# First transfers issued before the branch, rotary tables copied within SBUF, own blocks loaded after the weights, query products ordered by piece of tokens

## The reference

```python
u = rmsnorm(h, ln1_g)
z = u @ w_in                    # zb|zc|zv (3 x 1024), q_lat 768, kv_lat 512, k_rope 64, gates 2 x 2048
y_conv = (zb * causal_dwconv3(zc * zv, conv_w)) @ w_conv_out
q = (rmsnorm(q_lat, q_a_g) @ w_q_b)       # 16 heads of 128 + 64
k, v = (rmsnorm(kv_lat, kv_a_g) @ w_kv_b) # 16 heads of 128 and 128, k_rope shared by the heads
q, k = rope(rmsnorm(q)), rope(rmsnorm(k)) # cos and sin of position * inverse frequency
h = h + (sigmoid(ga) * y_conv + sigmoid(gb) * causal_attention(q, k, v) @ w_mla_out) @ w_o
h = h + (silu(a_g) * a_u) @ w_down,  a = causal_dwconv3(rmsnorm(h) @ w_up) + b
```

## Time and profile before

| | us |
|---|---|
| median of 3 runs | 2425.15 |
| the profiled execution | 2420.54 |
| its span on the slowest core, 6 | 2418.9 |
| TensorE busy in it | 2350.9 (97%) |
| VectorE, ScalarE busy | 1342.5 (56%), 1094.9 (45%) |
| granted clock of TensorE, mean over core 6's span | 0.996 |

### The profile page before, as it was taken

The page is one execution under the profiler, slowest core; times in us unless marked ns, Lnnn a source line. Parts: engine busy times, 40 slices in busy tenths (PEclk is TensorE's granted clock), DMA queues, the critical chain, the costliest instruction groups (busy, mean ns, idle before and its releaser), DMA issues.

```text
span 2418.9 us, 41748 instructions; the slowest of 8 cores (2401.0 to 2418.9 us)
## 1 busy us (share of the span) xinstructions
PE 2350.9 (97%) x13850; PEld 1245.6 (51%) x13900; DVE 1342.5 (56%) x2585; ACT 1094.9 (45%) x1876; POOL 172.8 (7%) x330
## 2 busy tenths in 40 slices
PE   4989999999999999999999999999999999999999
PEld 2875555555555555544444444444444444444444
DVE  3772777777777777761111111277467457547742
ACT  4863788888788888861111113433023113213310
POOL 1000000000000000000000000000100100110011
PEclk9999999999999999999999999999999999999999
DMA  8654121212020202144554466454454455455457
GB/s 210 177 96 79 20 40 24 40 19 50 14 50 14 50 10 50 51 98 90 83 82 80 83 136 160 70 88 78 75 92 81 74 91 88 68 90 88 79 107 155
DMA packets 66053, 189.10 MB, mean 78 GB/s; under 512 B 7520, under 2 KB 23136, under 8 KB 64672
## 3 DMA queue, kind: packets, MB, share of 16 engines
q0 software_dynamic: 46944, 140.56, 35.5%
q1 hardware_dynamic: 18880, 45.67, 5.5%
HBM read 311.80 MB, written 14.51 MB: 135 GB/s over the span
## 4 chain that ended last, share of the span: by engine, by line
PE 94%; DMA 2%; DVE 1%; issue 1%; ACT 1%; SPq 0%; DVEq 0%; ACTq 0%; POOLq 0%
PE ps L612 94%; ACT arena L619 1%; DMA arena<-wkvin 1%; DMA arena<-wall 1%; DVE arena L630 1%; DVE arena L626 1%; SPq L646 0%; SPq L205 0%; ACT L619 0%; DVEq L183 0%; ACTq L183 0%; DVE arena L643 0%; SPq L210 0%; POOLq L183 0%; SPq L212 0%
## 5 line engine op out<-in xcount | busy, mean ns | idle before, releaser
L612 PE MATMUL ps<-arena 128*128 128x476 bf16 (+5 forms) x13850 | 2350.9, 331 | 63.7 <-DMA arena<-xg 18.9
L612 PEld LDWEIGHTS ps<-arena 128*128 128x128 bf16 x13900 | 1245.6, 98 | 1168.8 <-issue 79.6
L630 DVE TENSOR_TENSOR arena<-arena 128x478 f32<-128x478 f32 (+19 forms) x1292 | 640.8, 537 | 224.5 <-ACT arena L619 202.0
L630 DVE TENSOR_TENSOR arena<-ps,arena 128x476 f32<-128x476 f32 (+6 forms) x558 | 330.0, 591 | 770.2 <-PE ps L612 745.2
L619 ACT ACTIVATE arena<-arena 128x476 f32<-128x476 f32 (+9 forms) x543 | 378.1, 712 | 682.0 <-DVE arena L630 603.7
L619 ACT ACTIVATE arena<-ps,arena 128x476 bf16<-128x476 f32 (+6 forms) x832 | 491.2, 632 | 406.8 <-PE ps L612 373.6
L626 DVE SCALAR_TENSOR_TENSOR arena<-arena 128x476 f32<-128x476 f32 (+8 forms) x603 | 358.0, 609 | 47.0 <-ACT arena L619 25.4
L619 ACT ACTIVATE arena<-ps 128x512 bf16<-128x512 f32 (+7 forms) x496 | 268.3, 561 | 119.8 <-PE ps L612 116.1
L646 POOL DMA_DIRECT2D arena<-wall x302 | 159.4, 528 | 2112.0 <-PE ps L612 2048.0
L626 DVE SCALAR_TENSOR_TENSOR arena<-ps,arena 128x256 bf16<-128x256 f32 (+1 forms) x65 | 26.9, 464 | 5.2 <-ACT arena L619 4.1
L646 POOL DMA_DIRECT2D arena<-xg x23 | 12.7, 563 | 119.1 <-PE ps L612 53.5
(11 more groups left out here) (3 smaller groups left out, 0.3 us busy)
## 6 DMA issues: line engine op xcount, KB each, us to landing
arena<-wall POOLq DMA_DIRECT2D x182, 512.0 KB, 5.4
arena<-wall POOLq DMA_DIRECT2D x48, 320.0 KB, 4.2
arena<-xg SPq DMA_DIRECT2D x9, 1024.0 KB, 9.1
arena<-wall POOLq DMA_DIRECT2D x32, 256.0 KB, 3.9
arena<-xg POOLq DMA_DIRECT2D x15, 512.0 KB, 9.2
arena<-xo SPq DMA_DIRECT2D x16, 477.0 KB, 13.9
outT<-arena SPq DMA_DIRECT2D x31, 238.0 KB, 5.2
arena<-wall POOLq DMA_DIRECT2D x32, 224.0 KB, 5.6
```

Source lines behind the costliest of these rows:

```text
L612: S.add(PE, lambda e: e.matmul(out, lhsT=lhsT, rhs=rhs, start=start, stop=stop), reads, writes, cost=max(width(rhs) / 2400.0, 0.055) + 0.003)
L630: S.add(DVE, lambda e: e.tensor_tensor(out=out, in0=in0, in1=in1, op=op), reads, writes, cost=dcost(out, in0, in1) + held)
```

## The change

Five things change.

1. `cst`, the first seven chunks of `wkvin` (SyncE) and the eight pieces of pair 0 (GpSimd) are marked `pre` and issued ahead of the read of `which`. They must be the same in all shares, so the tile of pair 0 now lies at the start of the region and the staging tiles behind it. `posg`, which differs by share, follows after the branch, with chunk 7.
2. The tables are copied from `tS` and `tC` straight into `CS`, 16 transfers of 32 partitions each (4 quarters x 4 groups of rows). `cs_d` is gone. `rope(g)` waits only for the quarters it reads.
3. `oload(0)` and all later own blocks are asked for once chunk 15 of `wkvin` has been. The first two weights of ring `A` are asked for by `prefetch`, when the first `NST` own blocks have been asked for, and their transfers wait until the last of those has landed.
4. Query products go by pieces: blocks 0 to 3 of piece 0, of piece 1 and so on, then blocks 4 and 5; each reads only the columns of `u_own` of its piece (`Tup`). `krstat` of the last pair, and `kvstat` when the number of pairs is odd, move in among them, and the convolution begins when all query products are done. Small tiles are placed ahead of the later x tiles.
5. `NXB` (tiles for pairs) becomes 2 where a share has late own blocks (share 0), and the cap on `NST` rises from 6 to 7. By the sizes, share 0 goes from 4 and 5 tiles to 2 and 7; share 1 keeps 4 and 5, share 2 keeps 4 and 4, share 3 keeps 3 and 4.

```diff
@@ Sched.replay
-    def replay(self, e, eng, eng_sem, chan_sem, final_waits):
+    def replay(self, e, eng, eng_sem, chan_sem, final_waits, pre=False):
         for o in self.ops[e]:
+            if o.pre != pre:
+                continue
@@ emit
     def body(e, eng):
+        progs[0][0].replay(e, eng, eng_sem, chan_sem, (), pre=True)
         v = eng.value_load(which[0:1, 0:1])
@@ the first transfers
-    dma(SP, posi, posg[:, 0:QW], "pos", writes=[Tposi])
     dma(SP, cst, cstd[:, 0:NC_CONST - 128], "cst", writes=[Tcst])
...
-    for k in range(8):
-        if k < NWS:
-            wload(k)
-        if k % 2:
-            for h in range(2):
-                xpiece(0, h, 4 * (k // 2), 4)
+    for k in range(7):
+        wload(k)
+    for k in range(4):
+        for h in range(2):
+            xpiece(0, h, 4 * k, 4)
+    for e in (SP, POOL):
+        for o in S.ops[e]:
+            o.pre = True
+    dma(SP, posi, posg[:, 0:QW], "pos", writes=[Tposi])
+    if NWS > 7:
+        wload(7)
@@ sine, csload
         act(dst, q, AF.Sin, [Tq], [Tdst])
-        x = 1 - which
-        dma(SP, cs_d[128 * x:128 * x + 128, 0:QW], dst, "csw%d" % x, reads=[Tdst], writes=[Tcsd[x]])
-        if which == 0:
-            return
-        csload(0, 1)
-        oload(0)
-
-    def csload(q0, q1):
+        F1.mark("sin", which)
+
+    def csload(q):
 
         for r in (2, 3, 0, 1):
-            x = 0 if r < 2 else 1
-            dma(SP, CS[32 * r:32 * r + 32, QW * q0:QW * q1].rearrange("p (q n) -> p q n", n=QW),
-                cs_d[128 * x + 32 * q0:128 * x + 32 * q1, 0:QW].rearrange("(q p) n -> p q n", p=32), "cs%d%d" % (q0, r),
-                reads=[Tcsd[x]], writes=[TCSall[4 * (q0 > 0) + r]])
-        F1.mark("tab", q0)
+            v, Tv = (tC, TtC) if r < 2 else (tS, TtS)
+            dma(SP, CS[32 * r:32 * r + 32, QW * q:QW * q + QW], v[32 * q:32 * q + 32, :], "cs%d%d" % (q, r),
+                reads=[Tv], writes=[TCSall[4 * q + r]])
+        F1.mark("tab", q)
@@ units of the first stage
-        if i > 0:
+        if 0 < i < 5:
+            for q in [i - 1] if sh.first else range(4) if i == 1 else ():
+                f_d.units.append(Unit(lambda q=q: csload(q), 0.0, pos=-9.0, ok=lambda q=q: at("sin") >= 1 and (q == 0 or at("old") >= 0)))
+        if True:
             f_d.units.append(Unit(lambda i=i: oload(i), 0.0, pos=-9.0,
-                                  ok=lambda i=i, g=g, c=c: (not c or at("ld%d" % (g - 1)) > 0) and at("old") >= i - 1 and at("own") >= i - NST
+                                  ok=lambda i=i, g=g, c=c: at("w") >= 15 - NWS and (not c or at("ld%d" % (g - 1)) > 0) and at("old") >= i - 1 and at("own") >= i - NST
                                   and at("cast") >= sh.ncast[max(i - NST + 1, 0)] - 1))
-        if i == 1:
-            f_d.units.append(Unit(lambda: csload(1, 4), 0.0, pos=-9.0, ok=lambda: at("ld%d" % min(3, NG - 1)) > 0 and at("tab") >= 0))
@@ buffers, prefetch
-    NXB = 4 if spare > 7 else 3
-    NST = min(spare - NXB, 6)
+    NXB = 2 if sh.late else 4 if spare > 7 else 3
+    NST = min(spare - NXB, 7)
...
+    def prefetch():
+
+        wlimit["A"] = 2
+        wbehind.extend(t for t in Txo[min(NST, len(sh.own)) - 1:] if not t.dead)
+        wpump()
+        wbehind.clear()
@@ query products
-    def ql(i, t):
+    qseq = [(i, t) for b in (range(4), range(4, 6)) for t in range(NT) for i in b]
+
+    def ql(m):
+        i, t = qseq[m]
...
-            mm(PS[p][:, 0:n], wv[:, k, :], u_own[:, k, 2 + off:2 + off + n], k == 0, k == 15, [Tw, Tu[k]], [TP[p]])
+            mm(PS[p][:, 0:n], wv[:, k, :], u_own[:, k, 2 + off:2 + off + n], k == 0, k == 15, [Tw, Tup[k][t]], [TP[p]])
...
     NQ = 6 * NT
     for n in range(NQ):
-        if n == 4:
+        if n == 2 and NG % 2:
+            st_l.units.append(Unit(lambda: kvstat(NG - 1), 0.45, need=[Tsqkv[2 * ((NG - 1) % 2) + 1]], pos=-9.0))
+        if n == 5:
+            st_l.units.append(Unit(last_krstat, 0.12, need=[Tsqkr[(NG - 1) % 2]], pos=-9.0))
             st_l.units.append(Unit(krot, 0.0, pos=-9.0))
```

More of the change, by code:

```diff
@@ L645, in dma @@
     def dma(eng, out, in_, chan, reads=(), writes=()):
[L646 to L647 removed]
+        o = S.add(eng, lambda e: e.dma_start(out=out, in_=in_), reads=reads, writes=writes, chan=chan,
+                  cost=in_.shape[0] * width(in_) * esz(in_.dtype) / 2.7e5)
+        if o:
+            o.where = repr((out, in_))
     def rsq(out, ssq, n, reads, writes):
```

113 lines of the change are left out of this document (68 added, 45 removed).

## The result

The changed kernel is slower, not faster. Its time is that of the kernel before times 1.0028, with a 95% interval of 1.0016 to 1.0039, so about 7 us lost where I forecast 4 gained. The other five lie between 2427.4 and 2431.6, with a median of 2430.8.

The account below looks back on a forecast made before the run. TensorE's products were taken as the work, with only idle time to save, mainly in the front that ScalarE's chunk scaling ends. Front 2.6 plus query products 1.2 made 3.8 us off 2425.15: 2421 us, range 2412 to 2429.

Parts of the forecast that it names:

- Of 7.9 us of lead 2.6 are left: Front, core 6: transfers start 7.9 us sooner, but sines waiting for `posg` leave a gain of 2.6 us.
- 1.2 us gained: Query products, core 6: placed between the last pair's two statistics, they remove TensorE's 1.16 us wait; 1.2 us gained.
- `posg` begun at 9.7, landed at 22: Front, SyncE's queue: `posg` begun at 9.7 us, asked for at 12.3, landed behind seven chunks at 22.
- rival 3: Branch: the far share's code is fetched through full queues, `posg` lands at 29.9, 4.1 us slower, 2429; chance 0.15.
- under the wait: Front: squares of pair 0, its mean square and a 1.28 us table change hidden while ScalarE waits for the sines.
- The last chunk at 42.5: Front, ScalarE: sines at 30.4 and 36.4 us, last `wkvin` chunk scaled at 42.5 instead of 45.1.
- It follows at a fixed distance: End of front: with the last chunks scaled, TensorE has all operands of its first pair and follows at a fixed distance.
- nothing loses: Own blocks behind the weights: `oload(0)` some 9 us sooner, pair loads move no more than the last chunk; 0 us.
- Tables without DRAM: 0, own blocks: nothing: Front: 832 KB less traffic against six more issues, 2.5 us of SyncE's time; both costed at nothing, as were own blocks.
- The hole at 134 us: 0: TensorE's idle stretch from VectorE's queue of own blocks: left unchanged, 0, with 8.1 us the most it could give.
- Rival 4: Hole at 134 us: the front's 2.6 us are waited away there and only 1.2 stay, 2424; chance 0.15.
- Rival 2: Front: `posg` overtakes the chunks or lands near 15 us, the full 7.9 us arrive, 2416 or 2414; chance 0.25.

Follow-up runs that it names:

- experiment 9: Changed kernel with the squares of the query products put in the buffers in turn, not in their piece's buffer: ratio 1.0008 [0.9998, 1.0018], 2424.4 us.
- nine other kernels with the same beginning: Nine follow-up kernels that begin like the changed kernel, first transfers ahead of the read of `which`; `posg` asked for at 16.6 to 20.9 us on core 6.
- experiment 3: Kernel before with only the first transfers moved ahead of the read of `which`, `posg` after the branch: ratio 1.0014 [1.0003, 1.0025], 2427.1 us.
- experiment 1: Changed kernel with `which` read first, then the shared first transfers, still ahead of the branch: ratio 1.0040 [1.0025, 1.0054], 2432.5 us.
- experiment 5: Changed kernel with both sines on ScalarE behind the last of the sixteen scaled chunks: ratio 0.9978 [0.9967, 0.9989], 2417.7 us.
- the four kernels of the second table: Changed kernel; kernel before with early transfers alone; changed kernel with old query order; changed kernel with squares in turn: 100th weight load 10.9 to 11.4 us after last chunk.
- experiment 4: Changed kernel with the old order of query products, their banks, and the last pair's statistics back in the first stage: ratio 1.0003 [0.9992, 1.0014], 2424.8 us.
- experiment 2: Changed kernel without its first part: transfers back behind the branch, `posg` first, the rest kept: a single time, 2425.3 us, no interval.
- experiment 12: Kernel before with both sines behind the sixteen chunks: ratio 1.0027 [1.0015, 1.0039], 2430.1 us.
- experiment 13: Kernel before with the first transfers ahead of the branch and both sines behind the chunks: two times, 2421.3 and 2422.5 us, no interval.
- experiment 14: Changed kernel with first transfers back behind the branch, sines behind the chunks, squares in turn: ratio 0.9980 [0.9969, 0.9991], 2416.7 us.
- the first four rows of the table: Changed kernel as is, with squares in turn, with sines last, and with both: +7.5, +3.6, -7.1, -6.4 us against the kernel before at weight load 100.
- experiment 8: Changed kernel with `which` first, old query order, pair 1 asked for sooner, and whole `posg` among the first transfers: ratio 0.9968 [0.9954, 0.9981], 2414.4 us.
- experiment 10: Changed kernel with both sines behind the chunks and the squares of the query products in turn: ratio 0.9952 [0.9938, 0.9967], 2410.4 us.

## Why the prediction was wrong, point by point

Two steps of the sum failed. "Of 7.9 us of lead 2.6 are left" was about -1.9 us (experiment 9, ratio 1.0008, with an interval that reaches to none), and "1.2 us gained" by the query products was -5. The time lies nearly 2 us above my range.

**The lead itself.** Right: the first chunk was asked for at 1.52 us (forecast 1.6), `xg` at 1.56. SyncE was through with its chunks at 7.8, not 4.5: issues of 0.42 us grew to 1.63 as the queue filled. That is 3.3 us of the loss of `posg`.

**`posg` begun at 9.7, landed at 22.** From the load of `which` to the first issue in the branch I took the 5.2 us of empty queues; it was 22.43 - 7.82 = 14.6, and the landing was at 26.7. In this execution 8.1 of the 9.4 us that were added are in the read of `which` (9.38 - 1.33) and 1.4 in the jump (4.71 - 3.34). With the 3.3 us above, less the 2.58 us stall of the first issue that didn't come (0.33 now), that makes the 10.1 us between 12.3 and 22.43. In the nine other kernels with the same beginning it is the other way round: in eight of them the read grew by 0.6 to 2.2 us, and the stretch from its end to `posg` more, from 3.8 to between 6.3 and 8.0. So rival 3, the far branch through full queues, had a real mechanism, and I gave it 0.15. What it added to the read of `which` it didn't name. Its threshold, a landing at 25.8, was not what decides: experiment 3 loses 3 us with a cast at 24.9.

By the rule weighed there (the Trainium skill, "Advanced Engine Details and Errata", Control Flow Timing, about 108 ns for a compare-and-branch) the jump would be next to nothing; the trace disagrees again, with 4.71 us.

**The cast follows the landing.** I had VectorE start when `posg` is there. But the sum of pair 0's squares now stands ahead of the cast in its order, and waits for pair 0's last pieces. In experiment 1, and in six of the nine kernels above, the cast waits for that sum and not for `posg`. I had said that squares, mean square and table change lie "under the wait". Only the mean square does: the squares hold the cast, sums of squares put between make the 8.4 us to the angle 9.3 (26.82 to 36.16), and the table change of 1.28 us comes when the angle is there and adds to the chain. So the first sine ran at 37.46 in the profiled execution and at 34.43 in experiment 9, not at 30.4.

**The last chunk at 42.5.** It was 48.8 in the profiled execution and 44.6 in experiment 9. The chain was the right one, ScalarE's fixed order, as experiment 5 shows; its inputs were off.

**"It follows at a fixed distance", and "nothing loses".** This is the step that failed in kind. I took the last chunk as the end of the front, had TensorE follow it at the old distance, and let the pair loads move "by no more than the last chunk does". The distance grew from 7.1 us to about 11 in the four kernels of the second table with the lead and the sines between the chunks, also where the last chunk came sooner than before: in experiment 4 it is done 1.5 us sooner, and the 100th weight load 2.8 us later. While the sines hold the chunks, no chunk is reloaded and pair 1 isn't asked for, so the DMA engines, nearly full until 30 us, run almost empty until 40; all that follows, chunks, own block 0, copies and pair 1, then wants them at once, and TensorE waits 3.9 to 5.4 us for pair 1. I had priced the sines by the chunks behind them and not by the transfers. What the wait for pair 1 costs by itself stays open: no run takes it away with the chunks in time. After that wait TensorE's granted clock is lower as well (0.77 between 48 and 58 us and 0.93 until 81; before it was 1.00): the 184 products behind it take 21.58 us, where 196 took 21.22 before. That is about 1.7 us, an estimate from these two rows.

**Tables without DRAM: 0, own blocks: nothing.** Not refuted as the sines stood, in the time: experiments 3 and 4 differ by 3 us in favour of these parts, which is inside the uncertainty. But without the lead TensorE waits for pair 1 as well (experiment 2). With the sines late on purpose they are worth about 11 us (experiments 12 to 14).

**Query products by piece: 1.2 us gained.** The sign was wrong. The wait of 1.16 us did go, but three of 0.8 us came, and in all the order cost 5 us. I looked at banks and weights, not at the buffer of the squares: one for each piece, fine while the pieces alternate.

**The hole at 134 us: 0.** Right within what can be seen. Its longest wait changed from 5.65 to 3.71 us with small waits around it; those that TensorE's timeline lists between 130 and 157 us come to 8.4 us before and 8.0 after. In the first four rows of the table no more than 1.2 us is lost or won between n = 100 and 1000. In experiment 4, though, 4.3 us are lost there, and 3.0 won in experiment 8. Rival 4 is out: a gain in front is kept to the end (experiments 5 and 10).

**Rival 2, the full lead.** It is what experiments 10 and 14 show, about 7 us, when nothing holds the chunks. Not by `posg` landing early, as I had it: there the sines simply come last.

**Share 1.** I had it end near 2407 us, with the first sine at 28.6 and the last chunk at 39. On core 1 they came at 35.0 and 46.9, and it ended at 2416.6. That share 2 stayed the slowest was right, but not for the reason given.

## What to carry to other kernels

A transfer moved to the front helps only as far as the next thing in a fixed order lets it: look for what stands between the items of the moved stream, here two sines, and ask what their inputs do. Then ask what the DMA engines do meanwhile. When they bound the front, a stretch in which they run empty is the loss, whenever the last chunk comes. Small reads of control values that were cheap in empty queues are not cheap behind bulk transfers, so price them at the traffic that they will meet. When the order of products changes, count the products between a buffer's write and its read anew; a buffer for each piece is enough only while the pieces alternate.

## What the runs showed of the hardware

On core 6 the read of `which` took 0.87 + 0.46 us in the kernel before and 8.23 + 1.15 behind sixteen transfers. In nine other kernels with the same beginning it took 1.9 to 7.4 us in all, so it differs much from one execution to the next. From its end to `posg` it took 3.8 us in quiet queues, 5.2 in the changed kernel and 6.3 to 8.0 in the nine others. On core 0, whose code comes first, it was about 0.3 us in both kernels, up to the issues at 2.77 and 11.95. So it is the jump to a far share that costs, and it costs more behind the first transfers.

The rows alone don't say what the jump waits for. The Trainium skill ("Runtime: NRT & Kernel Launch", Instruction fetch mechanics) says that a taken branch to a target outside the two pages at hand has to fetch the page by DMA first. That fits: the jump to the first program is short, the one to the third is long, and longer behind the first transfers. No run here shows the fetch itself. The same page of the Trainium skill (The ~15µs preamble/postamble breakdown) gives the load of registers from HBM at a launch as about 1.3 us; the two loads of the kernel before were shorter (0.87 and 0.46), and the first one behind the transfers was 8.23.

Small copies from SBUF to SBUF are not quick in this traffic. Here are the transfers of core 6 after, asked for between 34 and 75 us (count, KB each, median us from issue to landing), beside SyncE's timeline:

```profile
arena<-xg SPq DMA_DIRECT2D x4, 1024.0 KB, 19.4
...
arena<-arena SPq DMA_DIRECT2D x16, 104.0 KB, 13.0
```

```profile
22.82 18.10 SPq L655 DMA_DIRECT2D arena<-wkvin  x9
40.97 0.42 SPq L655 DMA_DIRECT2D arena<-xg  x1
41.44 12.99 SPq L655 DMA_DIRECT2D arena<-arena  x16
```

The copies took 13.0 us to land, two thirds of what own blocks ten times as large took in the same stretch (19.4), and 12.99 / 16 = 0.81 us each to issue, twice the 0.42 of the own block just ahead of them.
